# Expert layers on one core: the round's results are put back one step later

## The reference, cut to what matters

```python
hid = silu(einsum('td,edf->tef', xt, w_gate[g])) * einsum('td,edf->tef', xt, w_up[g])
hid = hid * gates[:, g, :, None]
out = out + einsum('tef,efd->td', hid, w_down[g])      # summed over all experts
```

## Time and profile before

| | us |
|---|---|
| median of three runs | 2490.31 |
| the profiled execution | 2492.87 |
| its span, first to last instruction | 2491.0 |
| TensorE busy in the span | 2269.3 |

### The profile page before, as it was taken

How to read it: one execution, slowest core, us unless ns; L and a number is a source line. 1 busy time by engine, 2 the same in 40 slices (tenths; PEclk the granted TensorE clock), 3 DMA queues, 4 the chain that set the end, 5 groups by cost and what they waited for, 6 DMA issues and landing times. The chain is left out here.

```text
span 2491.0 us, 40588 instructions
## 1 busy us (share of the span) xinstructions
PE 2269.3 (91%) x17537; PEld 1349.7 (54%) x17537; DVE 859.7 (35%) x1712; ACT 413.7 (17%) x747; POOL 22.4 (1%) x114
## 2 busy tenths in 40 slices
PE   5979999799988999998998899999998899899996
PEld 3759888464447678666443455444443455444442
DVE  6875776641114121324111262132111352131112
ACT  1023432010001000221000123121000224021001
POOL 0000000000000000000000000000000000000000
PEclk9989999889999999999999999989999999999999
DMA  9900000789996665216999533466999443567995
GB/s 377 336 1 4 3 4 4 276 323 421 421 419 254 236 220 187 84 71 243 421 421 419 190 129 119 185 239 238 420 421 397 142 132 118 187 239 300 420 421 232
DMA packets 139922, 602.21 MB, mean 242 GB/s; under 512 B 34840, under 2 KB 37976, under 8 KB 84960
## 3 DMA queue, kind: packets, MB, share of 16 engines
q1 hardware_dynamic: 126912, 591.66, 60.7%
q10 hardware_dynamic: 12576, 7.89, 1.1%
q0 software_dynamic: 256, 0.02, 0.0%
HBM read 598.46 MB, written 1.05 MB: 241 GB/s over the span
## 5 line engine op out<-in xcount | busy, mean ns | idle before, releaser
L2361 PE MATMUL ps<-store 128*32 128x512 f32 (+1 forms) x2816 | 319.6, 607 | 26.6 <-DMA store<-in_moe_w_up 14.4
L3056 PE MATMUL ps<-store,x_features 128*128 128x512 f32 x704 | 322.7, 602 | 4.8 <-PEq L2879 2.6
L403 PE MATMUL ps<-store 128*128 128x512 f32 x480 | 216.3, 612 | 11.0 <-PEq L752 7.9
L2361 PEld LDWEIGHTS ps<-store 128*32 128x32 f32 x2816 | 89.3, 112 | 249.0 <-issue 249.0
L3056 PEld LDWEIGHTS ps<-store,x_features 128*128 128x128 f32 x704 | 128.3, 192 | 136.4 <-issue 134.3
L2379 PE MATMUL ps<-store 128*32 128x512 f32 (+1 forms) x1408 | 160.2, 595 | 36.2 <-DVE store L2484 36.2
L2319 PEld LDWEIGHTS ps<-store 128*128 128x128 f32 x1408 | 162.1, 193 | 42.9 <-issue 33.5
L2479 DVE TENSOR_TENSOR store<-ps,store 128x256 f32<-128x256 f32 x44 | 18.7, 425 | 480.8 <-ACT store L2427 480.8
L2319 PE MATMUL ps<-store 128*128 128x128 f32 x1408 | 170.5, 279 | 6.1 <-DVE store L2458 6.1
L433 PE MATMUL ps<-x_features,store 128*128 128x256 f32 x768 | 166.8, 379 | 0.9 <-PEq L752 0.9
L403 PEld LDWEIGHTS ps<-store 128*128 128x128 f32 x480 | 93.8, 197 | 129.6 <-issue 129.5
(11 more groups left out here) (434 smaller groups left out, 2296.7 us busy)
## 6 DMA issues: line engine op xcount, KB each, us to landing
store<-in_moe_w_gate SPq DMA_DIRECT2D x64, 1024.0 KB, 18.9
store<-in_moe_w_up SPq DMA_DIRECT2D x64, 1024.0 KB, 21.0
store<-in_moe_w_down SPq DMA_DIRECT2D x64, 1024.0 KB, 23.1
store<-in_w_exp_gate SPq DMA_DIRECT2D x64, 1024.0 KB, 16.7
store<-in_w_exp_up SPq DMA_DIRECT2D x64, 1024.0 KB, 18.6
store<-in_w_exp_down SPq DMA_DIRECT2D x64, 1024.0 KB, 20.0
store<-in_ada_w SPq DMA_DIRECT2D x48, 1024.0 KB, 13.6
store<-in_w_in SPq DMA_DIRECT2D x40, 1024.0 KB, 5.0
```

What stands on the lines that cost most here:

```text
L403: mm = pe.matmul(k.ps[:, set_ * 4 + tile * 2 + h, 0:n], xT[:, s, tile * P:(tile + 1) * P], w[:, kk, c0:c0 + n], start=(s == 0), stop=(s == ...
L2361: mm = pe.matmul(v3(k.ps[w * CAP:(w + 1) * CAP, 6, :], 2, F), xe[:, q % 2, s, w], both[:, :, s * F:(s + 1) * F], start=(s == 0), stop=(s = ...
L3056: mm = pe.matmul(k.ps[:, 2 * (j % 2) + tile, :], x, row[:, 0:HALF], start=(s_ == 0), stop=(s_ == K8 - 1))
```

## The change

Putting back is taken out of its place behind `second_layer` of the same round. `scatter(q - 1)` now stands between `turn(q)` and `second_layer(q)`; after the last round `scatter(10)` follows by itself. `gatedT` gets a third buffer, as it is needed for one round longer, and two waits move: `second_layer` waits for the copies of `out` of the round before only in the last round, and `take_tokens(q)`, which writes the same banks 4 and 5, waits for the copies of round q - 2.

```diff
-    gatedT = v3(c.take(2 * T), 2, T)
+    gatedT = v3(c.take(3 * T), 3, T)
...
             def take_tokens(q):
 
                 wait_pair(pe, k.slots_built, q)
+                if q > 1:
+                    wait_pair(pe, k.out_moved0, q - 2)
+                    wait_pair(pe, k.out_moved1, q - 2)
...
             def second_layer(q):
 
                 wait_pair(pe, k.hidden_moved, q)
-                if q:
+                if q == ROUNDS - 1:
                     wait_pair(pe, k.out_moved0, q - 1)
                     wait_pair(pe, k.out_moved1, q - 1)
...
-                        pe.matmul(k.ps[:, 2 * tile + h, :], gatedT[:, q % 2, tile * P:(tile + 1) * P],
+                        pe.matmul(k.ps[:, 2 * tile + h, :], gatedT[:, q % 3, tile * P:(tile + 1) * P],
...
                 turn(q, True, q + 1 < ROUNDS)
+                if q:
+                    scatter(q - 1)
                 second_layer(q)
-                scatter(q)
...
+            scatter(ROUNDS - 1)
             overflow(pe, general)
...
-                vec.tensor_copy(gatedT[:, q % 2], k.ps[:, 7, T:2 * T]).then_inc(k.gated_moved.sem, 1)
+                vec.tensor_copy(gatedT[:, q % 3], k.ps[:, 7, T:2 * T]).then_inc(k.gated_moved.sem, 1)
```

## The result

The changed kernel takes 2494.61 us, the kernel before 2484.53 (medians of 20 runs each, 2487.82 to 2499.04 and 2477.63 to 2492.50). The ratio is 1.0038, 95% interval 1.0029 to 1.0047: slower by 9.4 us by the ratio, 10.1 by the medians. The two profiled executions have spans of 2492.4 and 2491.0 us, only 1.4 apart, since the stages between the expert phases are not the same in each execution: from the end of the first phase to F of the next one the kernel before took 405.4 us at a granted clock of 0.97, the changed one 398.9 at 0.98. So the traces are compared stage by stage.

The account below looks back on a forecast made before the run. The DMA queue was taken to bound each phase up to round 9's first layers, TensorE's work from there; 7.1 us longer ends plus 1.7 us clock, 8.8 us on the median 2490.31, gave 2499.1 us, range 2494 to 2507.

Parts of the forecast that it names:

- F: Short name for the first layers of a round on TensorE, which wait for the DMA of up weights.
- The clock adds to it: At round 9's first layers, a longer DMA wait lowers the clock in one phase of four: 1.7 us, bounds 0 and 6.8.
- so the lateness stays: After each phase's end, following work starts from that end, so the added 7.1 us over four phases is kept.
- The queue sets F of round 9: Up to round 9's first layers, blocks at 421 GB/s set the pace, 22.4 us against 18.35, so earlier gains become waiting.
- The rival of a real gain: Expert phases: if blocks were not the bound, closed holes save 34 to 40 us, near 2453; chance 5%.
- surely fall: Wait before F of round 9: if round 8 ran at full clock, 1.7 us longer, and the clock surely falls.
- The longer end: F of round 9 to closing turn: one added C less two closed holes, 1.78 us a phase, 7.1 in four.
- C: Short name for the putting back of a round on TensorE, 3.63 us in the profiled round before.
- S: Short name for the second layers of a round on TensorE, before which the hole of 0.85 us stood.
- The added time goes on the median: Whole time: the added 8.8 us is put on the median of 2490.31 us, giving 2499.1.
- The moved wait and the register loads: Taking's wait for out_moved costs nothing; register loads before F taken as 0 of 0 to 6.8 us.

Follow-up runs that it names:

- Only the end changed: Kernel before, with the new order only from the putting back of round 8 on: 1.0053 of before, 13.2 us over.
- the half blocks: Blocks of rounds 2 to 10 load half their bytes, in both orders: old order 0.9854 of before (2447.70 us), new order 0.9674 (2402.33 us).
- its repetition: The changed kernel measured again beside other runs, nothing else changed: 1.0032 of before, 8.0 us over.
- the split: Kernel before, with the taking of tokens split: first half ahead of the turns, second between turns and second layers; 1.0014 of before, 3.5 us over.

## Where the prediction was wrong, and why, and where it was right

The forecast of 2499.1 us was 4.5 us too high. The difference, 8.8 us forecast and 9.4 measured, came out near by luck: terms that were wrong in both directions made it up. The step that failed first is in "The clock adds to it": the wait before F of round 9 "grows by 0.99, to 2.5, 2.35, 2.25 and 2.25 us", so "one fall in four: 1.7 us". The profiled execution had waits of 5.38, 4.12, 5.20 and 2.37 us and three falls, 5.6 us. The second is "so the lateness stays": 1.62 us of it did not.

- *What held.* The queue sets F of round 9: holes gone, waits for DMA grown to 66.2 us (55 to 75 was forecast), F of round 9 where the blocks put it, its last up block landing at the same distance from the phase's start. The waits begin in round 4 in two phases (0.74 and 0.88 us), not in 5 or 6. "Only the end changed" and the half blocks show it from both sides. The rival of a real gain (34 to 40 us) comes true, at 45, when the blocks are made smaller, and only then.
- *The clock* is the term most under-sized. I counted one slow F of round 9 in four and 1.7 us; the profiled execution had three, of 2.6, 1.7 and 1.3 us over 7.07, 5.6 in all, and its repetition two, 4.2 in all. The step that failed is that F of round 8 stays slow as before. The wait ahead of it changed too, so it often ran at full clock (7.07 at 697.69), and then the wait ahead of round 9 is 4.1 to 5.5 us. Where F of round 8 was slow, the wait was 2.16 to 2.37 us, as forecast, and F of round 9 ran at full clock. I had written the other case down ("surely fall") and given it no weight in the sum. The Trainium skill (TensorE: Matmul & The Clock Gate, Loop structure matters more than you think) names a long DMA wait between matmuls as what brings the slow clock. The traces here agree for every wait of 4.0 us and more, as in "only the end changed" in all four phases, and for none under 2.47.
- *The longer end* was 1.53 us a phase, not 1.78, 6.1 us in place of 7.1: a round without waits saves 1.25 us and not 0.99, since C to S and S to F (3.53 and 3.46 us) are tighter than S to C and C to F (3.57 and 3.63).
- *What I left out* is the queue at the end of the first phase. "The lateness stays" is wrong there: 1.62 us of it went into a wait for SyncE, which the list of TensorE's waits shows under a sequencer's name and not a DMA's.
- *The sum* by these rows is 6.1 + 5.6 - 1.6 = 10.1 us in the profiled execution and 6.1 + 4.2 - 1.6 = 8.7 in the repetition, against 7.1 + 1.7 = 8.8 forecast. The clock term was too small by 2.5 to 3.9 us; the end, too large by 1.0, and the 1.6 at the queue took that back.
- *The level* failed. "The added time goes on the median" took 2490.31, a median of three runs, as the time of before; over 20 runs it is 2484.53, 5.8 lower. So 2499.1 was 4.5 too high while the difference was 0.6 off, and the measured 2494.61 lies at the very foot of my range, which was drawn from that level with 5 us below the forecast. Three runs that spread over 5.7 us cannot carry a range of 13; the scatter of the level belonged in it.
- *The moved wait and the register loads* cost nothing, as said: F starts 3.46 us behind S with no gap, and the DMA rate is unchanged (420 GB/s over 600 to 720 us, before 421).

## What to carry to other kernels

Where a queue paces a stage, count a change on the engine only from the last awaited transfer to the stage's end: all that is saved before it turns into waiting, and work that is put off across that wait comes on top, here 1.53 us a phase after what it fills. The useful direction is the reverse: work that needs no weights goes ahead of the last wait, which together with the split (0.9 by itself) made the end 1.9 us shorter than before. And look at what else waits at a stage's end; here it was the engine that issues the DMAs.

## What the runs showed of the hardware

- A wait of TensorE can cost more than its length. In all twelve profiles F took 7.07 us behind every DMA wait under 2.47 us, and 8.4 to 10.0 us behind every one of 4.0 us and more, 8.77 the commonest. Between 2.47 and 4.0 it goes either way (2.47 and 2.53 slow before, 2.47 and 2.54 in the changed kernel at full clock; in the split 3.88 at full clock and 3.97 slow). The granted clock over such an F was 0.73 (9.66 us), over one of 7.05 us 1.00.
- Matmuls that compute nothing can fill such a wait. 18 of them ahead of F of round 8 left waits of 1.0 to 1.3 us, and that F ran at 7.07, in all four phases; behind 11 of them and waits of 2.8 to 3.0 it took 8.6 to 8.8. The two kernels differ in the issue at the end of the first phase too.
- Closing a hole can raise the clock's price elsewhere: a slow F of round 8 shortens the wait ahead of round 9, a fast one lengthens it (2.37 behind 8.85 us, 5.38 behind 7.07).
- 1 MiB blocks moved at 419 to 421 GB/s in whole slices in both kernels. Late in a phase one issue of such a block can hold SyncE for over 2 us (2.37 at 756.67), where others take 0.43; I read this as a full queue.
- The scatter of this kernel, some 15 us over 20 runs of the kernel before, is larger than the effect of the change. The distance from F of round 0 to F of round 9 repeats to some 0.4 us wherever the blocks alone set it (183.8 to 184.2 in the kernel before and the changed one).
